# Loading a token block by column halves and splitting the copies of its turned tiles between two engines

## The chip, the core and the metric

The kernel runs on one core of one Trainium2 chip. The metric is the device time of one launch in microseconds (us). Five engines work beside each other and meet through semaphores: TensorE (PE, matmuls and weight loads), VectorE (DVE), ScalarE (ACT), GpSimd (POOL) and SyncE (SP), which here only issues transfers. Matmul results land in eight banks (bank 0 to 7) that DVE and ACT read.

## The reference

One inference step of a two-layer encoder for 256 prompt tokens and 64 sample tokens, 320 in all, of width 1024 (float32):

```python
x = [x_prompt (256, 1024); x_sample (64, 1024)]
for i in range(2):
    h = rmsnorm(x, ln_mix_pre[i])                   # x / sqrt(mean(x^2) + eps) * g
    mix = attention(h @ w_att_in) @ w_att_out       # i = 0: forgetting and window attention
    mix = mlstm(h @ w_rec_in) @ w_rec_out           # i = 1
    x = x + rmsnorm(mix, ln_mix_post[i])
    x = x + rmsnorm(conv_ffn(rmsnorm(x, ln_ffn_pre[i])), ln_ffn_post[i])
    x = x + sigmoid(x @ w_ple_gate[i]) * (p[i] @ w_ple[i])
```

Only the first step matters here: x comes in by rows (tokens), is turned so that features lie on the partitions, is multiplied by the norm's gain, and meets the first columns of w_att_in. The factor 1/sqrt(mean) is applied later, to the results of the matmuls.

## The kernel before

**Data.** The turned x, `xT`, is eight tiles j = 0 to 7 of 128 features by 320 tokens. Every float32 product is made of three faster ones: an operand is split into a high part (`hH` for x times gain, `wh` for weights) that ACT writes as a rounded copy, and a low part (`hL`, `wl`) that DVE gets by subtracting. A weight *unit* is 1024 by 128 numbers (512 KB) in one of R = 4 slots: SP loads it into `raw`, ACT makes `wh` (`hi(u)`), DVE makes `wl` (`lo(u)`), then PE uses it for 24 matmuls.

**The start.** SP issues three loads of x into `xtok` (tokens on the partitions, whole rows of 4 KB, all counted by `ld_x`), then unit 0, unit 1 and so on; unit u waits for `lo(u-4)`. ACT issues five small loads of the norms' gains (`nrow`). PE first does WARM = 16 throwaway matmuls on constants, then waits for all of x, and turns tile after tile (`turn_rows`, three transposes each, against an identity); between tile 1 and tile 2 it turns the gains (`parameters(1)`, which waits for `nrow`), and behind each of the tiles 3 to 7 stand three more throwaway matmuls. DVE copies each turned tile from its bank to `xT` (`x_in(j)`) and the gains to `NC` (`par_in(1)`). ACT multiplies (`hH`), DVE makes `hL` (`prenorm_lo`).

**The first projections.** `ahead` runs units 0 and 1 together, feature tile by feature tile k: four matmuls that need `hH[k]`, then two that need `hL[k]`; its first one needs `lo(1)`. Then come unit 2 (`in_unit`), inside which, before its k = 5, stands `stats`: matmuls that add up the squares of x over the partitions. It waits until DVE has added the squares of tiles 0 to 6 (`add_squares`), which ACT made with `Square`. From there DVE (`ms`), POOL (`rcol`, the inverse root), DVE (`diag`), PE (`spread_rms`, inside unit 3) and DVE (`rstd`) make the factor by which all results of the projections are multiplied.

**What sets the order.** Each engine's program is written out by hand and runs in its order; an instruction that waits holds up all behind it. ACT: `hi(0)`, four `hH`, `hi(1)`, four `hH`, `hi(2)`, four squares, `hi(3)`, four squares, the narrow weights `wnH` (which wait for a transfer of POOL's queue, whose first transfer waits for unit 2's landing), some small ones, `hi(4)`. DVE: the copies of tiles with `lo(0)` and `lo(1)` between them, eight `hL`, `lo(2)`, `lo(3)`, six additions of squares, `ms`, `lo(4)`, `diag`, `lo(5)`, `rstd`. The banks are given out by `group_banks`, in turn over banks 0 to 3 for these groups.

Of the kernel before, what the change touches and what calls it, by code (L numbers as in the profile page):

```python
# [21 lines left out]
P = 128  # L22
# [30 lines left out]
WARM = 16  # L53
# [78 lines left out]
def group_banks():  # L132

    fixed = {("pt_e", 7): 4, ("pt_o", 7): 5, ("pt_s", 7): 6}
    fixed.update({("o", s): 7 for s in range(8)})
    upper = ("rows", "spread", "W", "Y", "Cs")
    banks, turn, last, previous = [], [0, 0], {}, []
    for n, key in enumerate(group_order()):
        b = fixed.get(key)
        if b is None:  # L140
            k = int(key[0] in upper)
            b = 4 * k + turn[k] % 4
            turn[k] += 1
        banks.append(b)
        previous.append(last.get(b))
        last[b] = n
    return banks, previous
# [16 lines left out]
def encoder_step(nc, I, O):  # L164
    ctx = ExitStack()
    with ctx:
# [168 lines left out]
        for name, signal, n in (("x", "x_in", 8), ("pe", "pe_f", 4), ("in0", "in_read0", 18),  # L335
                                ("narrow0", "narrow_step0", 1), ("vt", "vt_read", 5), ("kt", "kt_read", 5), ("lf", "lf_read", 1),
                                ("pt_e", "pt_e", 8), ("pt_o", "pt_o", 8), ("pt_s", "pt_s", 8), ("o", "o_lo0", 8), ("in1", "in_read1", 24),
                                ("narrow1", "narrow_step1", 1), ("rows", "rows_read", 1), ("spread", "sdec", MH), ("W", "P", MH), ("ktok", "Kg", MH),
                                ("vtok", "vtok_read", 8), ("Y", "Yn", 12), ("Cs", "C_new", MH), ("Cp", "Cp", MH), ("heads", "mo_f", 8)):
            read_by(name, signal, n)  # L340
# [63 lines left out]
        def _(sp):  # L404
            sp.dma_start(xtok[:, 0, :], I["x_prompt"][0, 0:P]).then_inc(sem("ld_x"), 16)
            sp.dma_start(xtok[:, 1, :], I["x_prompt"][0, P:TP]).then_inc(sem("ld_x"), 16)
            sp.dma_start(xtok[0:TS, 2, :], I["x_sample"][0]).then_inc(sem("ld_x"), 16)
# [10 lines left out]
            for l in range(2):  # L418
                w_in, cols, w_out = (I["w_att_in"], ATT_COLS, I["w_att_out"]) if l == 0 else (I["w_rec_in"], REC_COLS, I["w_rec_out"])
                for i, c in enumerate(cols):  # L420
                    load(UNITS[f"in{l}"] + i, col_unit(w_in[0], c))
                for i in range(8):
# [232 lines left out]
        def _(pe):  # L655
# [83 lines left out]

            for i in range(WARM):  # L740
                mmul(bank[7][:, 0:P], ones[:], ident[:], start=True, stop=True)  # L741
            pe.wait_ge(sem("ld_x"), 48)
            for j in range(KT):
                gi = gid("x", j)
# [5 lines left out]
                if j >= 3:  # L750
                    for i in range(3):
                        mmul(bank[7][:, 0:P], ones[:], ident[:], start=True, stop=True)
# [408 lines left out]
        def _(act):  # L1161
# [69 lines left out]
            def input_attention():  # L1231
                for j in range(KT):
                    act.wait_ge(sem("x_in"), j + 1)
                    if j == 0:
                        act.wait_ge(sem("par_in"), 1)
                    A(hH[:, j, :], xT[:, j, :], ACT.Copy, scale=NC[:, 0, 64 + j:65 + j]).then_inc(sem("h_hi"), 1)
                    if j == 3:
                        hi(1)
# [231 lines left out]
        def _(dve):  # L1470
# [138 lines left out]
            def input_attention():  # L1609
# [5 lines left out]
                def x_in(j):  # L1615
                    gi = gid("x", j)
                    bank_full(dve, gi)
                    V.tensor_copy(xT[:, j, :], gbank(gi)[:, 0:T]).then_inc(sem("x_in"), 1)

                x_in(0)  # L1620
                x_in(1)
                par_in(1)
                x_in(2)
                x_in(3)
                lo(0)
                x_in(4)
                x_in(5)
                lo(1)
                x_in(6)
                prenorm_lo("mixpre0", 0, 0, 64)  # L1630
                x_in(7)
                for j in range(1, 8):
                    prenorm_lo("mixpre0", 0, j, 64)
# [357 lines left out]
```

## Time and profile before

| | us |
|---|---|
| median of three runs | 1091.24 |
| lowest and highest | 1090.67 and 1092.66 |
| the profiled execution | 1091.82 |
| its span, from the first instruction to the last | 1090.1 |
| PE busy | 1073.3 |
| DVE busy | 674.6 |
| ACT busy | 534.9 |
| POOL busy | 253.5 |

The span is what the rows of the profile cover; 1.7 us of the profiled execution lie around it. Times in rows count from the span's start. A PE that is busy is not always at its full rate, since a matmul's row also covers its wait in the pipeline.

### The profile page before, as it was taken

Reading aid. Unit: us, or ns where it says so; the run is one execution under the profiler, and the core shown is the slowest. Engines: PE = TensorE matmul, PEld = TensorE weight load, DVE = VectorE, ACT = ScalarE, POOL = GpSimd, SP = SyncE. Lnnn points to the kernel's source line nnn. Section 1 sums busy time; section 2 is a strip of 40 time slices with the busy share of each in tenths; the row PEclk is TensorE's granted clock in tenths of the full one; section 3 lists DMA queues with packets and bytes.
Section 4 is the critical chain, followed back from the end, with each engine's and each line's share of the span. In section 5 each row is a group of like instructions: output and inputs, shape, how many; then the busy total and the mean of one; then the engine's idle time right before and its main releaser. Section 6 shows DMA issues by size and latency. Waiting matters only on the chain.

```text
span 1090.1 us, 20380 instructions
## 1 busy us (share of the span) xinstructions
PE 1073.3 (98%) x7343; PEld 1043.8 (96%) x7343; DVE 674.6 (62%) x1232; ACT 534.9 (49%) x932; POOL 253.5 (23%) x384
## 2 busy tenths in 40 slices
PE   9999999999999999999999999999999999999998
PEld 8889989999999999999999889899999999999998
DVE  5876547777777753334876655567777777433364
ACT  5465455555555543334656444545555555433353
POOL 5600036222333210002410102432223332100020
PEclk9999999999999999999999999999999999999999
DMA  9623252555555545554555334355555555455441
GB/s 238 169 72 98 87 155 72 169 156 164 146 151 154 153 141 152 155 152 126 136 148 135 97 100 127 103 113 159 162 163 144 148 153 153 143 152 152 149 122 50
DMA packets 281926, 150.39 MB, mean 138 GB/s; under 512 B 5592, under 2 KB 278816, under 8 KB 281872
## 3 DMA queue, kind: packets, MB, share of 16 engines
q1 hardware_dynamic: 279184, 144.20, 47.0%
q0 software_dynamic: 2544, 5.40, 1.7%
q8 instruction: 37, 0.61, 0.2%
q14 instruction: 17, 0.14, 0.0%
q10 hardware_dynamic: 144, 0.05, 0.0%
HBM read 145.54 MB, written 4.08 MB: 137 GB/s over the span
## 4 chain that ended last, share of the span: by engine, by line
PE 94%; DVE 3%; POOL 2%; ACT 1%; issue 0%; DVEq 0%; POOLq 0%; ACTq 0%
PE bank L662 27%; PE bank L664 27%; PE bank L663 27%; PE bank L686 2%; PE bank L689 1%; PE bank L704 1%; PE bank L1038 1%; DVE wl L1481 1%; PE bank L726 1%; DVE hidden_lo L1944 1%; PE bank L712 1%; PE bank L741 1%; PE bank L929 1%; POOL sqb L393 1%; PE bank L890 0%
## 5 line engine op out<-in xcount | busy, mean ns | idle before, releaser
L1481 DVE TENSOR_TENSOR wl<-raw,wh 128x1024 fp32r<-128x1024 f32 x270 | 332.4, 1232 | 253.2 <-ACT wh L1178 251.3
L662 PE MATMUL bank<-hH,wh 128*128 128x320 f32 x1280 | 399.7, 312 | 1.1 <-DVE mix L1530 1.0
L664 PE MATMUL bank<-hH,wl 128*128 128x320 f32 x1280 | 396.1, 309 | 0.0
L663 PE MATMUL bank<-hL,wh 128*128 128x320 f32 x1280 | 396.0, 309 | 0.0
L1178 ACT ACTIVATE wh<-raw 128x1024 fp32r<-128x1024 f32 x270 | 284.4, 1055 | 190.6 <-PE bank L664 175.1
L662 PEld LDWEIGHTS bank<-hH,wh 128*128 128x128 f32 x1280 | 240.7, 188 | 4.6 <-issue 2.7
L663 PEld LDWEIGHTS bank<-hL,wh 128*128 128x128 f32 x1280 | 240.8, 188 | 0.0
L664 PEld LDWEIGHTS bank<-hH,wl 128*128 128x128 f32 x1280 | 240.8, 188 | 0.0
L662 PE MATMUL bank<-hidden_hi,wh 128*128 128x320 f32 x720 | 223.4, 310 | 0.5 <-ACT mix L1369 0.5
L664 PE MATMUL bank<-hidden_hi,wl 128*128 128x320 f32 x720 | 222.5, 309 | 0.0
L663 PE MATMUL bank<-hidden_lo,wh 128*128 128x320 f32 x720 | 222.5, 309 | 0.0
L662 PEld LDWEIGHTS bank<-hidden_hi,wh 128*128 128x128 f32 x720 | 135.1, 188 | 1.3 <-ACT mix L1369 0.8
L663 PEld LDWEIGHTS bank<-hidden_lo,wh 128*128 128x128 f32 x720 | 135.2, 188 | 0.0
L664 PEld LDWEIGHTS bank<-hidden_hi,wl 128*128 128x128 f32 x720 | 135.1, 188 | 0.0
L635 POOL TENSOR_TENSOR fb<-cv,us 128x256 f32<-128x256 f32 x64 | 44.3, 692 | 312.4 <-DVE us L1924 188.9
L393 POOL TENSOR_TENSOR sqb<-sqb 128x320 f32<-128x320 f32 x42 | 43.4, 1034 | 203.8 <-ACT sqb L1420 146.2
L1405 ACT ACTIVATE cv<-cv 128x322 f32<-128x322 f32 x64 | 30.3, 474 | 99.7 <-DVE cv L1919 99.7
L1919 DVE SCALAR_TENSOR_TENSOR cv<-gp,PC,cv 128x322 f32<-128x322 f32 x128 | 70.6, 552 | 7.8
L1409 ACT ACTIVATE hidden_hi<-fb 128x320 f32 (+1 forms) x64 | 30.2, 472 | 78.2 <-POOL cs L639 78.2
L639 POOL COPY cs<-gp 128x4 f32 x64 | 62.0, 968 | 0.0
L1928 DVE TENSOR_TENSOR hidden_lo<-fb,hidden_hi 128x320 f32 (+1 forms) x64 | 31.4, 490 | 43.4 <-ACT hidden_hi L1409 43.4
L1402 ACT ACTIVATE cv<-gp,PC 128x322 f32<-128x322 f32 x64 | 42.1, 658 | 26.5 <-DVE gp L1911 26.1
(374 smaller groups left out, 1060.0 us busy)
## 6 DMA issues: line engine op xcount, KB each, us to landing
raw<-in_w_ffn_up SPq DMA_DIRECT2D x128, 512.0 KB, 4.1
raw<-in_w_ffn_down SPq DMA_DIRECT2D x64, 512.0 KB, 3.9
raw<-in_w_rec_in SPq DMA_DIRECT2D x24, 512.0 KB, 3.9
raw<-in_w_att_in SPq DMA_DIRECT2D x18, 512.0 KB, 4.9
raw<-in_w_ple_gate SPq DMA_DIRECT2D x16, 512.0 KB, 4.1
raw<-in_w_att_out SPq DMA_DIRECT2D x8, 512.0 KB, 3.7
raw<-in_w_rec_out SPq DMA_DIRECT2D x8, 512.0 KB, 3.9
raw<-in_w_ple SPq DMA_DIRECT2D x4, 512.0 KB, 3.5
```

The lines of the kernel that those rows point to most:

```text
L393: ops.tensor_tensor(sqb[:, 0, :], sqb[:, 0, :], sqb[:, j, :], ALU.add).then_inc(sem("sq_added"), 1)
L635: g.tensor_tensor(fb[:, s, 0:TP], cv[:, s, 0:TP], us[:, s, 0:TP], ALU.mult)
L639: g.tensor_copy(dst, tail).then_inc(sem(f"f{l}"), 1)
L662: mmul(out, a, rh[:, k, :], start=first, stop=False)
L663: mmul(out, a, rl[:, k, :], start=False, stop=False)
L664: m = mmul(out, b, rh[:, k, :], start=False, stop=last)
L1178: A(wh[:, u % R, :], raw[:, u % R, :], ACT.Copy).then_inc(hi_ready, 1)
L1402: A(cv[:, s, :], gp[:, s, 2:T + 4], ACT.Identity, scale=PC[:, l, bass.ds(j + 64, 1)], bias=PC[:, l, bass.ds(j + 96, 1)]).then_inc(sem(f"cv ...
L1405: A(cv[:, s, :], cv[:, s, :], ACT.Gelu_apprx_tanh).then_inc(sem(f"gelu{l}"), 1)
L1481: V.tensor_tensor(wl[:, u % R, :], raw[:, u % R, :], wh[:, u % R, :].bitcast(F32), ALU.subtract).then_inc(lo_ready, 1)
L1919: V.scalar_tensor_tensor(out=cv[:, s, :], in0=gp[:, s, tap:tap + T + 2], scalar=PC[:, l, bass.ds(j + 32 * tap, 1)], in1=cv[:, s, :], op0=A ...
L1928: V.tensor_tensor(FL[:, bass.ds(j, 1), :].rearrange("p a t -> p (a t)"), fb[:, s, :], FH[:, bass.ds(j, 1), :].rearrange("p a t -> p (a t)" ...
```

## The change

- x is loaded by halves of its columns. SP issues both prompt blocks' first 512 columns as one load and the sample's as another (`ld_x0`), then unit 0, then the other halves (`ld_x1`), then unit 1. Rows are now 2 KB long. PE waits for the first half before tile 0 and for the second before tile 4.
- WARM goes from 16 to 9. Behind tiles 4 to 7 stand two throwaway matmuls each, behind tile 3 none: 8 in place of 15. They write bank 3 in place of bank 7.
- The turned tiles use banks 4 to 7 (tile j in bank 4 + j % 4), a tile waiting for the copy of the tile four before it. The first projections keep their banks 1, 2, 3 and 0.
- DVE copies the even tiles (`x_even`), ACT the odd ones (`x_odd`). On both engines the copies now stand among `hi`, `lo`, `hH` and `hL`; `hL` of tile 1 is made before tile 6 is copied.

```diff
-WARM = 16
+WARM = 9
...
+    fixed.update({("x", j): 4 + j % 4 for j in range(KT)})
...
-            sp.dma_start(xtok[:, 0, :], I["x_prompt"][0, 0:P]).then_inc(sem("ld_x"), 16)
-            sp.dma_start(xtok[:, 1, :], I["x_prompt"][0, P:TP]).then_inc(sem("ld_x"), 16)
-            sp.dma_start(xtok[0:TS, 2, :], I["x_sample"][0]).then_inc(sem("ld_x"), 16)
+            def load_x(half):
+                landed = sem(f"ld_x{half}")
+                c = slice(half * 512, (half + 1) * 512)
+                sp.dma_start(xtok[:, 0:2, c], I["x_prompt"][0].rearrange("(t p) d -> p t d", p=P)[:, :, c]).then_inc(landed, 16)
+                sp.dma_start(xtok[0:TS, 2, c], I["x_sample"][0][:, c]).then_inc(landed, 16)
...
+                if l == 0:
+                    load_x(0)
                 for i, c in enumerate(cols):
                     load(UNITS[f"in{l}"] + i, col_unit(w_in[0], c))
+                    if (l, i) == (0, 0):
+                        load_x(1)
...
-            for i in range(WARM):
-                mmul(bank[7][:, 0:P], ones[:], ident[:], start=True, stop=True)
-            pe.wait_ge(sem("ld_x"), 48)
+            def throwaway(n):
+                for i in range(n):
+                    mmul(bank[3][:, 0:P], ones[:], ident[:], start=True, stop=True)
+
+            throwaway(WARM)
             for j in range(KT):
+                if j % 4 == 0:
+                    pe.wait_ge(sem(f"ld_x{j // 4}"), 32)
                 gi = gid("x", j)
                 bank_free(pe, gi)
                 turn_rows(gi, T, lambda t, n: xtok[0:n, t, :], j)
                 if j == 1:
                     pe.wait_ge(sem("ld_norms0"), 16 * 5)
                     parameters(1)
-                if j >= 3:
-                    for i in range(3):
-                        mmul(bank[7][:, 0:P], ones[:], ident[:], start=True, stop=True)
+                if j >= 4:
+                    throwaway(2)
```

ACT's order at the start, before the change. `wh<-raw` is `hi`, `hH<-xT,NC` a tile times its gain:

```order
L1178 ACTIVATE wh<-raw 128x1024 [waits raw_landed0]
L1236 ACTIVATE hH<-xT,NC 128x320 [waits par_in,x_in]
L1236 ACTIVATE hH<-xT,NC 128x320 [waits x_in] x3
L1178 ACTIVATE wh<-raw 128x1024 [waits raw_landed1]
L1236 ACTIVATE hH<-xT,NC 128x320 [waits x_in] x4
L1178 ACTIVATE wh<-raw 128x1024 [waits raw_landed2]
```

The same place of the change, up to `hH` of tile 2; `xT<-bank5` and `xT<-bank7` are the copies of tiles 1 and 3:

```order
L1190 ACTIVATE wh<-raw 128x1024 [waits raw_landed0]
L1248 ACTIVATE xT<-bank5 128x320 [waits bank_done5]
L1252 ACTIVATE hH<-xT,NC 128x320 [waits x_even,par_in]
L1190 ACTIVATE wh<-raw 128x1024 [waits raw_landed1]
L1248 ACTIVATE xT<-bank7 128x320 [waits bank_done7]
L1252 ACTIVATE hH<-xT,NC 128x320 [waits x_odd]
L1252 ACTIVATE hH<-xT,NC 128x320 [waits x_even]
```

Behind these follow the copy of tile 5, `hH` of 3 and 4, the copy of tile 7, `hH` of 5, 6 and 7, and `hi(2)` as before. `hi(1)` moved from behind four `hH` to behind one, so ten instructions stand between it and `hi(2)` in place of four.

DVE's order before, from the copy of tile 3 on; `wl<-raw,wh` is `lo`, `hL<-xT,NC,hH` is `prenorm_lo`:

```order
L1618 COPY xT<-bank0 128x320 [waits bank_done0]
L1481 TENSOR_TENSOR wl<-raw,wh 128x1024 [waits hi_ready]
L1618 COPY xT<-bank1 128x320 [waits bank_done1]
L1618 COPY xT<-bank2 128x320 [waits bank_done2]
L1481 TENSOR_TENSOR wl<-raw,wh 128x1024 [waits hi_ready]
L1618 COPY xT<-bank3 128x320 [waits bank_done3]
L1485 SCALAR_TENSOR_TENSOR hL<-xT,NC,hH 128x320 [waits h_hi]
L1618 COPY xT<-bank0 128x320 [waits bank_done0]
L1485 SCALAR_TENSOR_TENSOR hL<-xT,NC,hH 128x320 [waits h_hi] x7
L1481 TENSOR_TENSOR wl<-raw,wh 128x1024 [waits hi_ready] x2
```

And in the change, from the copy of tile 0 on:

```order
L1646 COPY xT<-bank4 128x320 [waits bank_done4]
L1641 COPY NC<-bank0 128x96 [waits bank_done0]
L1509 TENSOR_TENSOR wl<-raw,wh 128x1024 [waits hi_ready]
L1646 COPY xT<-bank6 128x320 [waits bank_done6]
L1509 TENSOR_TENSOR wl<-raw,wh 128x1024 [waits hi_ready]
L1513 SCALAR_TENSOR_TENSOR hL<-xT,NC,hH 128x320 [waits h_hi]
L1646 COPY xT<-bank4 128x320 [waits bank_done4]
L1513 SCALAR_TENSOR_TENSOR hL<-xT,NC,hH 128x320 [waits h_hi]
L1646 COPY xT<-bank6 128x320 [waits bank_done6]
L1513 SCALAR_TENSOR_TENSOR hL<-xT,NC,hH 128x320 [waits h_hi] x6
L1509 TENSOR_TENSOR wl<-raw,wh 128x1024 [waits hi_ready] x2
```

Four copies left DVE's queue, and `lo(1)` stands ahead of the copies of tiles 4 and 6.

## Rows read from the trace of the kernel before

**Rows 1.** The page: busy time, and shares of the chain that ended last.

```profile
PE 1073.3 (98%) x7343; PEld 1043.8 (96%) x7343; DVE 674.6 (62%) x1232; ACT 534.9 (49%) x932; POOL 253.5 (23%) x384
PE 94%; DVE 3%; POOL 2%; ACT 1%; issue 0%; DVEq 0%; POOLq 0%; ACTq 0%
```

**Rows 2.** The chain in order of time: start, us, what.

```profile
2.10 6.63 PE bank L741 x32
...
10.95 0.86 PE bank L752 x6
11.82 0.42 PE bank L726 x3
```

**Rows 3.** Landings: the three loads of x, then unit 0, unit 1.

```profile
L407 SPq DMA_DIRECT2D xtok<-in_x_sample x1: 576/576/576, 1.7 to 1.7; - x1
...
DMA to landing us min/median/max: 3.9/5.1/6.5
...
L416 SPq DMA_DIRECT2D raw<-in_w_att_in x1: 578/578/578, 2.3 to 2.3; - x1
...
DMA to landing us min/median/max: 7.3/7.3/7.3
...
L416 SPq DMA_DIRECT2D raw<-in_w_att_in x1: 758/758/758, 3.0 to 3.0; - x1
...
DMA to landing us min/median/max: 8.5/8.5/8.5
```

**Rows 4.** Order of time, DVE: start, us, what, [idle before].

```profile
16.54 3.32 DVE L1485 SCALAR_TENSOR_TENSOR hL<-xT,NC,hH 128x320 fp32r<-128x320 f32 x7
19.78 2.35 DVE L1481 TENSOR_TENSOR wl<-raw,wh 128x1024 fp32r<-128x1024 f32 x2
22.05 3.48 DVE L393 TENSOR_TENSOR sqb<-sqb 128x320 f32<-128x320 f32 x6
...
29.64 0.79 DVE L1495 TENSOR_SCALAR cv<-ident,rcol 128x128 f32<-128x128 f32 x3 [0.79 <-POOL rcol L500]
...
32.14 0.49 DVE L1500 COPY rstd<-bank 128x320 f32<-128x320 f32 x1 [0.59 <-PE bank L712]
```

**Rows 5.** The same for ACT.

```profile
10.62 1.91 ACT L1236 ACTIVATE hH<-xT,NC 128x320 fp32r<-128x320 f32 x4
12.44 1.04 ACT L1178 ACTIVATE wh<-raw 128x1024 fp32r<-128x1024 f32 x1
...
17.13 1.05 ACT L1178 ACTIVATE wh<-raw 128x1024 fp32r<-128x1024 f32 x1
...
19.52 1.04 ACT L1178 ACTIVATE wh<-raw 128x1024 fp32r<-128x1024 f32 x1
...
24.91 0.31 ACT L1245 ACTIVATE wnH<-wnr 128x128 fp32r<-128x128 f32 x1 [2.90 <-DMA wnr<-in_w_rec_in]
...
26.55 1.99 ACT L1178 ACTIVATE wh<-raw 128x1024 fp32r<-128x1024 f32 x2
```

**Rows 6.** ACT's copy of a 128x320 result from a bank, later in layer 0.

```profile
L1229 ACT ACTIVATE hidden_hi<-bank x8: 417/424/438, 63.5 to 134.0; 128x320 fp32r<-128x320 f32 x8
```

**Rows 7.** Order of time, PE's weight loads: first of the projections, first of `stats`.

```profile
16.69 0.19 PEld L686 LDWEIGHTS bank<-hH,wh 128*128 128x128 f32 x1
...
25.89 1.45 PEld L704 LDWEIGHTS bank<-ones,sqb 128*128 128x128 f32 x12
```

**Rows 8.** Windows of 1 us: busy (count) of PE, PEld, DVE, ACT, POOL; PEclk, DMA, GB/s.

```profile
4.00:5.00 1.00, 1.00 (x6) 1.00 (x6) 0.00 (x0) 0.34 (x1) 0.78 (x4) 1.00 1.03 402
...
9.00:10.00 1.00, 1.00 (x7) 0.64 (x7) 0.73 (x2) 0.34 (x1) 0.00 (x0) 1.00 1.20 290
```

**Rows 9.** Throwaway matmuls from 2 to 7.75 us; then two windows of 3.4 us.

```profile
L741 PE MATMUL bank<-ident,ones 128*128 128x128 f32 x26 | 5.9, 427 | 2.1 <-POOL ones L476 2.1
...
161.60:165.00 3.40, 1.30 (x10) 0.90 (x8) 3.30 (x8) 2.48 (x7) 1.50 (x2) 1.00 0.38 113
165.00:168.40 3.40, 3.40 (x13) 3.40 (x14) 3.08 (x5) 2.76 (x8) 3.32 (x4) 0.50 0.02 5
```

More of the change, by code:

```diff
@@ L334, in encoder_step @@
             READ[gid("cache", i)] = ("cache_read", n + 1)
-        for name, signal, n in (("x", "x_in", 8), ("pe", "pe_f", 4), ("in0", "in_read0", 18),
+        for j in range(KT):
+            READ[gid("x", j)] = (("x_even", "x_odd")[j % 2], j // 2 + 1)
+        for name, signal, n in (("pe", "pe_f", 4), ("in0", "in_read0", 18),
                                 ("narrow0", "narrow_step0", 1), ("vt", "vt_read", 5), ("kt", "kt_read", 5), ("lf", "lf_read", 1),
@@ L1231, in input_attention, with x_odd, x_normed @@
             def input_attention():
[L1232 to L1235, printed above, removed]
-                    A(hH[:, j, :], xT[:, j, :], ACT.Copy, scale=NC[:, 0, 64 + j:65 + j]).then_inc(sem("h_hi"), 1)
-                    if j == 3:
-                        hi(1)
+                def x_odd(j):
+                    gi = gid("x", j)
+                    bank_full(act, gi)
+                    A(xT[:, j, :], gbank(gi)[:, 0:T], ACT.Copy).then_inc(sem("x_odd"), 1)
+                def x_normed(j):
+                    act.wait_ge(sem(("x_even", "x_odd")[j % 2]), j // 2 + 1)
+                    A(hH[:, j, :], xT[:, j, :], ACT.Copy, scale=NC[:, 0, 64 + j:65 + j]).then_inc(sem("h_hi"), 1)
+                x_odd(1)
+                act.wait_ge(sem("par_in"), 1)
+                x_normed(0)
+                hi(1)
+                x_odd(3)
+                x_normed(1)
+                x_normed(2)
+                x_odd(5)
+                x_normed(3)
+                x_normed(4)
+                x_odd(7)
+                for j in range(5, KT):
+                    x_normed(j)
                 hi(2)
@@ L1613, in par_in, with x_even @@
                     V.tensor_copy((PC, NC)[i % 2][:, i // 2, 0:n], gbank(gid("par", i))[:, 0:n]).then_inc(sem("par_in"), 1)
-                def x_in(j):
+                def x_even(j):
                     gi = gid("x", j)
                     bank_full(dve, gi)
-                    V.tensor_copy(xT[:, j, :], gbank(gi)[:, 0:T]).then_inc(sem("x_in"), 1)
-                x_in(0)
-                x_in(1)
+                    V.tensor_copy(xT[:, j, :], gbank(gi)[:, 0:T]).then_inc(sem("x_even"), 1)
+                x_even(0)
                 par_in(1)
-                x_in(2)
-                x_in(3)
                 lo(0)
-                x_in(4)
-                x_in(5)
+                x_even(2)
                 lo(1)
-                x_in(6)
                 prenorm_lo("mixpre0", 0, 0, 64)
-                x_in(7)
-                for j in range(1, 8):
+                x_even(4)
+                prenorm_lo("mixpre0", 0, 1, 64)
+                x_even(6)
+                for j in range(2, 8):
                     prenorm_lo("mixpre0", 0, j, 64)
```

## The prediction

> **What bounds the kernel now.** The page first: PE is busy for 1073.3 of the span's 1090.1 us and holds 94% of the chain that ended last [rows 1]. So time is won only where PE waits or does work that the result doesn't need. The chain in order of time shows such a place at the start: 16 throwaway matmuls from 2.10 for 6.63 us, then per turned tile 0.42 us of transposes, and from tile 3 on 0.86 us of throwaways for each [rows 2]. The first projection's weights load at 16.69 [rows 7]. All of x is in `xtok` at 1.7 + 6.5 = 8.2 [rows 3], just before the throwaways end (8.7), so at first sight PE's own queue sets the start, and the change shortens exactly that.
>
> The second look goes to what the projections need next. From the first projection to `stats` PE runs 25.89 - 16.69 = 9.20 us without a stop [rows 7]. `stats` needs DVE's six additions of squares, which end at 22.05 + 3.48 = 25.53 [rows 4]. PE comes to them 0.36 us after they are ready. That is all the lead the other engines have: if PE starts its projections x us sooner and the additions don't move, PE waits x - 0.36 us inside unit 2, and `rstd`, on which all results of the projections wait, is hardly sooner. So the question is not when PE starts, but when the additions end.
>
> **The change part by part, PE.** In the first 5.65 us 26 halves of throwaway matmuls start, 0.21 us each [rows 9] (a float32 matmul is two instructions; this is the half clock, 1.2 GHz, since later six take 0.86, 0.14 each [rows 2]). Nine matmuls, 18 halves: 3.8 us, so they end at 5.9. The first half of x is 640 KB; before, 512 KB had landed at 0.8 + 3.9 = 4.7 and 1 MB at 1.3 + 5.1 = 6.4 [rows 3], so it lands between 5.1 (by bytes) and 6.4. I take 5.9. Tiles 0 and 1 follow at once. The gains have no landing in the profile; their last load stands about beside unit 0's, which landed at 2.3 + 7.3 = 9.6, and I take that as the latest for them. Tiles 2 and 3 are then turned at 11.0 at the latest. The second half of x is complete when 1.25 MB of x and unit 0 are, the same bytes that were in at 9.6 before. Tiles 4 to 7 with two throwaways each take 0.42 + 0.57 = 1.0 us apiece at full clock: tile 7 is turned by 14.5, give or take 0.5, and PE is ready for the projections by then. It was 16.69.
>
> **ACT.** Here is what the change costs. `hi(1)` needs unit 1, which landed at 3.0 + 8.5 = 11.5 [rows 3]. The same 2.25 MB stand ahead of and in it in the change, so I leave it there. Before, ACT did four `hH` first and `hi(1)` at 12.44 didn't wait. Now it stands behind one `hH`, waits until 11.5, and behind it are queued seven `hH` and three copies. In a stream one `hH` takes (1.91 - 0.55)/3 = 0.45 us and one `hi` 1.99 - 1.05 = 0.94 [rows 5]. A copy from a bank is 0.42 long alone [rows 6] against `hH`'s 0.55, so I take 0.40 in a stream (bounds 0.33 and 0.45: 0.4 us over three). Sum: 11.5 + 0.94 + 3 x 0.40 + 7 x 0.453 = 16.8 for `hi(2)`. One wait comes on top: `hH` of tile 4 needs DVE's copy of it, which stands behind `lo(1)` and one `hL`: `hi(1)` ends at 12.54, `lo(1)` takes 1.13 and `hL` 0.46 in a stream [rows 4], the copy ends at about 14.7, and ACT would be there at 14.6. With 0.15 for it `hi(2)` starts at 16.95, in place of 17.13. The four squares and `hi(3)` keep their distance, 19.52 - 17.13 = 2.39: `hi(3)` ends at 16.95 + 2.39 + 1.04 = 20.4, before 20.56. So ACT, which had idled between `hH` for want of tiles, is now full, and gains 0.2 us only.
>
> **DVE.** It was bound by itself: `lo(3)` started at 19.78 + 1.13 = 20.91, 0.35 after `hi(3)` ended [rows 4, 5]. With four copies fewer it has its last `hL` behind it at about 18.3, `lo(2)` at 19.5, and waits for `hi(3)`. `lo(3)` starts at 20.5, the additions 1.14 later and end 3.48 after that: 25.1. PE loads the weights of `stats` at 25.15 in place of 25.89: **0.74 us sooner**.
>
> **What PE does meanwhile.** Its projections need `lo(1)`, over at 13.8, and start there, 2.9 us sooner than before; 9.2 later it is at `stats`, at 23.0, and waits 2.1 us. What the change says it does on PE is done, and three quarters of it is given back there.
>
> **Behind that.** `stats`, `ms`, `rcol`, `diag`, the nine blocks of matmuls ahead of `spread_rms`: all follow from `stats` and move with it. One tie is new if the gain is larger: `lo(4)` needs `hi(4)` (26.55 to 27.6), which stands behind `wnH`, which waited 2.90 us for its transfer until 24.91 [rows 5]. DVE waited 0.79 before `diag` and 0.59 before `rstd` [rows 4], 1.38 together. With `wnr` landing as before `rstd` can't come more than 1.4 us sooner, however early the squares are. For 0.74 the tie is slack. The bank moves cost nothing: the projections keep their banks and lose a wait.
>
> **Sum.** 1091.82 (the profiled execution, span and 1.7 around it) - 0.74 = 1091.1; against the median of the runs, 1091.24, it is 1090.5.
>
> **Rivals.**
> 1. *Loads late, ACT later still* (0.15). Every 0.1 us by which unit 1 lands later goes straight into the additions. x now comes in rows of 2 KB. Rows of 4 KB moved at 402 GB/s, weights' rows of 512 B at 290 [rows 8]. If 2 KB rows moved as slowly as the latter, 1.31 MB would take 4.5 in place of 3.3 us: unit 1 at 12.7, `stats` at 26.35, 0.5 us later than before: 1091.7. If a copy takes 0.45, add 0.15.
> 2. *Start carried through* (0.10). Unit 1 lands sooner (at the 402 and 290 GB/s of [rows 8], 2.36 MB would take 3.3 + 3.6 = 6.9 us and not the 8.5 from issue to landing, so there is some slack for another order of loads to find), and `wnr` too. Then 1.4 us with the tie, at most 2.9 with nothing in the way: 1089.8 to 1088.3. Against it: both must come together, and the bytes ahead of unit 1 are the same.
> 3. *Half clock* (0.15), the case that ends slower. Before, PE was busy without a break from 2.10, and up to 7.75 at least its matmuls kept the half clock's 0.21 us; and much later, after a stretch of 3.4 us in which it was busy for 1.30, the granted clock was 0.50 for the next 3.4 [rows 9]. In the change PE stops at 5.9 or after tile 1, while still at half clock. If it stays so, a tile takes up to 0.84 and two throwaways 0.84: from 9.6 or 10.5 tile 7 is turned at about 16.4 in place of 14.5, 1.3 after ACT wants to copy it, and the additions end at 26.4. The projections start near 17.3, and each us of them at half clock adds half a us. `stats` at 26.6 to 28.5: 0.7 to 2.6 later, middle 1.3: 1092.5. It decides from the point where PE starts its projections after 25.15 - 9.2 = 15.95, or tile 7 after 15.1; up to there the wait of 2.1 us swallows it (4 us of matmuls at half clock).
> 4. *Not what it says*: the first half lands no sooner than 8.2 (its sample part late, as before). Then tile 3 is turned by 11, tile 7 by 15.0, and the result is the forecast's.
>
> The Trainium skill (TensorE: Matmul & The Clock Gate, Part 4: PE-mode transpose) says that matmuls in transpose mode don't count as busy for the clock. By that rule the tiles would not help to raise it and rival 3 would be the likely case, 1092.5. In this trace PE did nothing but transposes from 8.7 to 10.9 (seven instructions in the window from 9 to 10 at a granted clock of 1.00 [rows 8]) and was not slowed; that speaks to keeping the clock, not to getting it. So I leave the rival at 0.15.
>
> **How the numbers follow.** Forecast (with rival 4) 0.60, rivals 1 to 3 0.15, 0.10, 0.15. Time 1090.5. Every mechanism moves less than 3 us of 1091, while three runs of one kernel spread over 2 us; 0.2%, 2.2 us, is about what can be told from no change. The range takes rival 2's tied end and rival 3's middle, and 0.5 us on either side for the runs' own spread: 1089.0 to 1093.0. Faster by over 0.2% needs rival 2 without the tie, or its tied end with luck in the runs: 0.10. Slower needs rival 3 at its far end: 0.10. Same: 0.80.
>
> **What would show it.** Right: transposes from about 6 us, ACT idle before `hi(1)` until 11.5 with a DMA as the releaser, projections from 13.8, PE idle some 2 us before `stats` with DVE's additions as the releaser, `lo(3)` waiting for ACT, `rstd` at 31.4. The first wrong step would show as a landing of unit 1 off 11.5, or as throwaways behind tile 4 still 0.21 apart. If PE doesn't wait at `stats`, the argument is wrong as a whole.

## The result, and the profile after

| | median us | range | runs |
|---|---|---|---|
| before | 1091.72 | 1090.35 to 1092.77 | 20 |
| changed | 1093.63 | 1091.86 to 1096.15 | 20 |

Ratio 1.0020, 95% interval 1.0013 to 1.0026: the change makes the kernel 0.2% slower. Forecast were 1090.5 us and a range of 1089.0 to 1093.0, so both missed.

The profiled execution of the changed kernel took 1092.07 us, with a span of 1090.4 in place of 1090.1. It is one of the quick ones of its 20. First the page, busy time and then the shares of the chain that ended last (compare [rows 1]).

```profile
PE 1071.8 (98%) x7315; PEld 1041.6 (96%) x7315; DVE 672.8 (62%) x1228; ACT 536.1 (49%) x936; POOL 252.8 (23%) x384
PE 93%; DVE 3%; POOL 1%; ACT 1%; DMA 1%; issue 0%; SPq 0%; DVEq 0%; POOLq 0%; ACTq 0%
```

PE does 28 instructions less (14 throwaway matmuls), yet nothing is won. A DMA is new in the chain. The chain in order of time (start, us, what) says which one, and stands against [rows 2].

```profile
3.21 7.39 DMA xtok<-in_x_sample
10.64 0.64 PE bank L735 x3
...
12.34 1.07 PE bank L751 x4
13.41 0.72 PE bank L735 x3
...
16.61 0.58 PE bank L695 x4
...
25.84 1.50 PE bank L713 x12
```

The start is now bound by a load: the second half of x. Behind it, `x3` of turned tiles take 0.72 us at 13.41, where [rows 2] have 0.42, and two throwaways 1.07. The landings, of that load and then of unit 1, the last line of each being us from issue to landing (compare [rows 3]):

```profile
L412 SPq DMA_DIRECT2D xtok<-in_x_sample x1: 682/682/682, 3.2 to 3.2; - x1
...
DMA to landing us min/median/max: 7.4/7.4/7.4
...
L421 SPq DMA_DIRECT2D raw<-in_w_att_in x1: 587/587/587, 3.9 to 3.9; - x1
...
DMA to landing us min/median/max: 8.2/8.2/8.2
```

So the second half of x was in at 3.2 + 7.4 = 10.6 and unit 1 at 12.1. Now stretches of the start, and one much later: busy us (count) of PE, PEld, DVE, ACT, POOL, then granted clock, DMA, GB/s (compare [rows 8, 9]).

```profile
2.00:5.60 3.60, 3.51 (x16) 3.51 (x17) 0.00 (x0) 1.28 (x1) 2.85 (x13) 1.00 0.93 272
5.60:8.20 2.60, 2.60 (x17) 1.61 (x15) 0.75 (x2) 0.34 (x1) 2.30 (x7) 1.00 1.09 338
8.20:10.60 2.40, 0.02 (x1) 0.00 (x0) 1.63 (x2) 1.49 (x3) 0.55 (x1) 1.00 1.17 255
10.60:12.40 1.80, 1.76 (x11) 1.29 (x12) 0.00 (x0) 0.24 (x1) 0.00 (x0) 1.00 1.20 290
12.40:15.80 3.40, 3.40 (x14) 2.62 (x14) 2.55 (x5) 3.24 (x7) 1.56 (x3) 0.50 1.11 269
15.80:26.00 10.20, 10.20 (x70) 9.86 (x70) 8.61 (x16) 9.14 (x22) 5.66 (x9) 1.00 0.98 250
162.60:169.40 6.80, 5.90 (x21) 5.50 (x22) 6.42 (x11) 6.09 (x17) 5.80 (x6) 0.50 0.02 6
```

Three readings. PE stands still from 8.2 to 10.6, with tiles 0 to 3 turned and tile 4 not there. Soon after, from 12.4, its granted clock is 0.50 (1.2 GHz) for 3.4 us. And near 165 us the kernel spends 6.8 us at half clock, where before it was 3.4 [rows 9]. Note the first row: the column says 1.00, but a matmul takes 3.51 / 16 = 0.22 us there; at the very start one has to read the durations.

What ACT and DVE do meanwhile (start, us, what, [idle before]); ACT first (compare [rows 5]), then DVE (compare [rows 4]), then PE's weight loads (compare [rows 7]).

```profile
12.16 1.06 ACT L1190 ACTIVATE wh<-raw 128x1024 fp32r<-128x1024 f32 x1 [2.47 <-DMA raw<-in_w_att_in]
...
17.70 1.04 ACT L1190 ACTIVATE wh<-raw 128x1024 fp32r<-128x1024 f32 x1
...
20.09 1.05 ACT L1190 ACTIVATE wh<-raw 128x1024 fp32r<-128x1024 f32 x1
```

```profile
21.17 1.23 DVE L1509 TENSOR_TENSOR wl<-raw,wh 128x1024 fp32r<-128x1024 f32 x1 [1.06 <-ACT wh L1190]
22.31 3.48 DVE L396 TENSOR_TENSOR sqb<-sqb 128x320 f32<-128x320 f32 x6
...
32.06 0.49 DVE L1528 COPY rstd<-bank 128x320 f32<-128x320 f32 x1 [0.68 <-PE bank L721]
```

```profile
16.34 0.19 PEld L695 LDWEIGHTS bank<-hH,wh 128*128 128x128 f32 x1
...
25.84 1.30 PEld L713 LDWEIGHTS bank<-ones,sqb 128*128 128x128 f32 x11 [0.26 <-DVE sqb L396]
```

ACT waits 2.47 us for unit 1 with its queue behind it, and DVE now waits for ACT, both as forecast. But the additions end at 25.79, where 25.53 was before. `stats` comes at 25.84 against 25.89, `rstd` at 32.06 against 32.14. This execution, then, has won 0.08 us up to `rstd`, and lost 0.4 later. That is not the loss of 1.9 us in the medians. The mean granted clock of the runs points to the rest: it was 0.990 or 0.992 in 14 of the 20 runs of the changed kernel, and in none of the 131 runs of before beside the experiments below (a 132nd, of 1161.0 us at 0.848, was in a slow state and is left out here and in the ratios). The profiled execution had 0.994. A mean of 0.992 instead of 0.997 is 0.005 x 1090 x 2 = 11 us more at half clock. The main question is where these lie, and which part of the change brings them.

The mean doesn't tell all. One of the 20 runs took 1095.38 us at 0.997, and such runs come back below: 3 of 10 at 1094.98 to 1095.35 in the second experiment, and 2 of 10 at 1094.99 and 1095.30 where the kernel before gets WARM = 9. All six have 9 throwaways ahead. The 71 runs of before at 0.997 end at 1092.49, and no other run at 0.997 took more than 1093.41. Since the column misses the half clock at the very start, a start that stays at half clock for longer would fit, but no profile fell on such a run: it stays open.

### The profile page after: what moved, and what is told of

Same layout as the page of the kernel before. It is cut to its first block, busy times and chain, and to the rows that moved or that the text cites. A ratio compares the mean times of both kernels' runs of the same rounds, so it can differ in the third digit from the quotient of the medians.

```text
span 1090.4 us, 20328 instructions
## 1 busy us (share of the span) xinstructions
PE 1071.8 (98%) x7315; PEld 1041.6 (96%) x7315; DVE 672.8 (62%) x1228; ACT 536.1 (49%) x936; POOL 252.8 (23%) x384
## 4 chain that ended last, share of the span: by engine, by line
PE 93%; DVE 3%; POOL 1%; ACT 1%; DMA 1%; issue 0%; SPq 0%; DVEq 0%; POOLq 0%; ACTq 0%
PE bank L671 27%; PE bank L673 27%; PE bank L672 27%; PE bank L695 2%; PE bank L698 1%; PE bank L713 1%; PE bank L1050 1%; DVE wl L1509 1%; PE bank L721 1%; DMA xtok<-in_x_sample 1%; DVE hidden_lo L1969 1%; PE bank L735 1%; PE bank L941 1%; POOL sqb L396 1%; PE bank L902 0%
```

## The experiments

Two theories. *Clock*: with fewer throwaways PE stops at the start before or shortly after it has the full clock, and then runs at 1.2 GHz through turned tiles and projections; the loads and copies matter little. *Loads*: x by halves lands late, and with it unit 1, so ACT and the additions come late; the throwaways matter little. All times are medians in us, with the ratio to the kernel before on the same chip. Each edit is against the changed kernel, unless a line says otherwise.

### The old throwaways in the changed kernel

```diff
-WARM = 9
+WARM = 16
-                if j >= 4:
-                    throwaway(2)
+                if j >= 3:
+                    throwaway(3)
```

> The changed kernel with the throwaway matmuls of before: 16 ahead of the tiles, 3 behind each of tiles 3 to 7. Loads, banks and copies stay changed. Theory A (the loss is the clock: PE stands still while it waits for x, falls to half clock, and the stop costs more than the shorter queue gains): PE is busy from 2.1 until the second half of x has landed, no stretch at half clock after about 8 us; projections start near 17.0, stats near 26.2, so 1092.0, at most 0.5 above the kernel before, and 1.5 below the changed one. Theory B (the loss is the later landing of unit 1, 12.16 in the profile after against 11.5, with more work queued behind it on ACT): throwaways don't matter, 1093.6 as the changed kernel.

Measured: 1092.78, ratio 1.0008 (0.9999 to 1.0017). The profiled run had no stretch at half clock up to 163 us, and the 11 runs had means of 0.994 to 0.997. Yet its second half of x landed at 11.4 and `hi(1)` started at 12.88, so that the additions ended at 26.33 and `stats` came at 26.39. The low mean clocks are gone, and of the 1.79 us that the changed kernel lost on this chip (1093.74 against 1091.95) 0.96 come back. How much is only roughly known: the interval overlaps that of the changed kernel beside it (1.0005 to 1.0023). What is left, 0.08%, isn't told from nothing by its interval.

### The new throwaways in the kernel before

```diff
# against the kernel before
-WARM = 16
+WARM = 9
-                if j >= 3:
-                    for i in range(3):
+                if j >= 4:
+                    for i in range(2):
```

> The kernel before with the throwaways of the change alone: 9 ahead of the tiles, 2 behind tiles 4 to 7. Theory A (clock): PE stands still from 5.9 until x lands at 8.2 and is at half clock for part of the start; 1093.3 to 1094.5, about as slow as the changed kernel or slower. Theory B (unit 1's landing and ACT's queue): loads and ACT are as before, seven throwaways less on PE can only help: 1090.7 to 1091.7.

Measured: 1094.13, ratio 1.0024 (1.0014 to 1.0033), without any of the new loads and copies. The windows of its profiled run, columns as above:

```profile
6.00:8.20 2.20, 0.77 (x5) 0.31 (x4) 0.00 (x0) 0.00 (x0) 1.97 (x6) 1.00 1.15 241
8.20:10.20 2.00, 2.00 (x12) 1.23 (x13) 1.64 (x4) 0.78 (x1) 0.58 (x1) 0.99 1.20 289
10.20:20.40 10.20, 10.20 (x39) 8.41 (x40) 8.29 (x16) 7.67 (x16) 7.10 (x11) 0.50 1.13 275
```

PE has little to do from 6.0 to 8.2, where it waits for x, and 2 us later it is at half clock for 10.2 us. `stats` came at 27.99 and `rstd` at 34.24, 2.1 later than before. Fewer throwaways alone can cost as much as the whole change. But this stop, before the first tile, is one that the changed kernel doesn't have: its first half was in at 5.2. The changed kernel's stop is at tile 4.

### The changed kernel once more

> The changed kernel as it is, for a second profile and on the same chip as the others. Both theories: 1093.6. Theory A: the profile shows a stretch at half clock in the first 20 us, perhaps at another place than the first profile's 12.4 to 15.8, and stats follows it; where the half clock lies later, stats comes later than the first profile's 25.8. Theory B: the stretch at half clock is at the same cost as before and stats stands at 25.5 to 26 whatever the clock does.

Measured: 1093.74, ratio 1.0014 (1.0005 to 1.0023); 7 of its 11 runs had a mean clock of 0.992. This time the profile fell on one of those. Its windows, then its chain:

```profile
6.50:9.90 3.40, 2.33 (x14) 1.30 (x13) 2.10 (x4) 1.83 (x3) 2.17 (x4) 1.00 1.12 316
9.90:13.40 3.50, 3.50 (x14) 2.60 (x15) 1.11 (x2) 1.93 (x4) 0.00 (x0) 0.50 1.20 290
13.40:20.10 6.70, 6.70 (x27) 5.80 (x27) 5.86 (x12) 5.37 (x12) 6.55 (x10) 0.50 1.15 292
20.10:28.00 7.90, 7.90 (x57) 7.90 (x55) 4.63 (x9) 6.49 (x15) 0.68 (x2) 1.00 0.67 158
```

```profile
3.20 6.58 DMA xtok<-in_x_sample
9.83 0.94 PE bank L735 x3
10.78 1.15 PE bank L751 x4
...
17.55 1.07 PE bank L695 x4
18.61 0.53 PE bank L698 x2
...
21.41 0.59 PE bank L695 x4
```

Here x came sooner than in the first profile (9.8 in place of 10.6), and ACT had unit 1 at 11.47, just as forecast. PE waited for the second half of x for 0.97 us only. The result is nevertheless worse: half clock for 10.2 us, 9.9 to 20.1. The same four matmuls of a projection take 1.07 at 17.55 and 0.59 at 21.41. The additions ended at 26.21, but PE came to `stats` only at 27.70, and `rstd` stood at 33.95, 1.8 later than before. At 1093.93 us this execution is of the medians' kind, and the first profile was a lucky one.

### Throwaways that fill the stop at tile 4

```diff
-                if j >= 4:
-                    throwaway(2)
+                if j >= 3:
+                    throwaway(8 if j == 3 else 3)
```

> The changed kernel with its PE idle time filled: 9 throwaways ahead of the tiles as in the change, 8 behind tile 3 (while the second half of x is awaited), 3 behind tiles 4 to 7. Theory A: the clock is kept wherever it had risen, projections near 16, stats at 25.8 or just ahead of it because ACT and the additions bind there: 1091.2 to 1092.0. Theory B: 1093.6 as the changed kernel.

Measured: 1093.04, ratio 1.0014 (1.0004 to 1.0023), a miss in size: by its times it isn't told from the unchanged kernel beside it, which has the same ratio. What it shows is on the clock: with 9 throwaways ahead as in the change, and only the stop at tile 4 filled, the profiled run kept the full clock to 163 us, and none of the 11 runs had a mean under 0.994 (the unchanged one beside it: 7 of 11 at 0.992). So it is what lies between tile 3 and tile 4 that brings the granted half clock, for executions like the second profile at least. (A third throwaway behind each later tile came with it. In the second profile the clock had already fallen at 9.9, so those can't be what would have kept it there; in the first it fell at 12.4, behind tile 4, and for that one they are not ruled out.) In its profile the start was late by the loads: the second half landed at 11.3, `hi(1)` started at 12.87, `stats` at 26.36, and `rstd` came at 32.58, 0.44 later than before. That is less than half of the 1.09 us between the medians, and 4 of the 11 runs took 1093.97 to 1095.21 at means of 0.994 or 0.995. What those lost isn't shown.

### The loads, one by one

```diff
# against the first experiment: each row of x whole, as before
-            def load_x(half):
...
+            sp.dma_start(xtok[:, 0, :], I["x_prompt"][0, 0:P]).then_inc(sem("ld_x"), 16)
+            sp.dma_start(xtok[:, 1, :], I["x_prompt"][0, P:TP]).then_inc(sem("ld_x"), 16)
+            sp.dma_start(xtok[0:TS, 2, :], I["x_sample"][0]).then_inc(sem("ld_x"), 16)
...
-                if j % 4 == 0:
-                    pe.wait_ge(sem(f"ld_x{j // 4}"), 32)
+                if j == 0:
+                    pe.wait_ge(sem("ld_x"), 48)
```

> The changed kernel with the throwaways of before (16, and 3 behind tiles 3 to 7) and the loads of before (three loads of whole rows of x ahead of unit 0). What stays changed are the banks, the copies on two engines and the place of hi(1). Theory C (splitting the loads makes unit 1 land later, and that went into the additions of squares): unit 1 lands at 11.5, hi(2) starts at about 17.0 and the additions end at 25.1 as the prediction worked out; PE's own queue then sets stats at 25.9, so 1091.7 to 1092.0, the kernel before's time. Theory D (the copies on ACT and hi(1)'s place are late whatever the loads do): the additions end at 26 or later, 1092.5 and more.

Measured: 1093.0, ratio 1.0008 (0.9999 to 1.0017), the same as with halves, and by its median what theory D says. Five runs lay at 1091.4 to 1092.0 and six at 1093.0 to 1093.6. The profiled run, one of the lower, had `hi(1)` at 11.12, the additions over at 25.50 (theory C had 25.1) and `rstd` at 31.77. What separates the two groups stayed open.

The other way round, only the loads by halves, in the kernel before:

```diff
# against the kernel before
+                if l == 0:
+                    load_x(0)
                 for i, c in enumerate(cols):
                     load(UNITS[f"in{l}"] + i, col_unit(w_in[0], c))
+                    if (l, i) == (0, 0):
+                        load_x(1)
```

> The kernel before with the loads by halves alone (first halves, unit 0, second halves, unit 1), PE waiting for each half; throwaways, banks and copies as before. Theory C: unit 1 lands at 12.2 to 12.9 as in the profiles of the changed loads; hi(1) stood at 12.44 on ACT anyway, so at most 0.5 later; 1091.7 to 1092.3. If instead the halves cost nothing, unit 1 at 11.5 and 1091.9.

Measured: 1091.71, ratio 0.9998 (0.9990 to 1.0007). The loads alone cost nothing, where the old order of ACT and 16 + 15 throwaways stand over them.

### ACT's order: `hi(1)` behind three more pieces

```diff
# against the first experiment
                 x_normed(0)
-                hi(1)
                 x_odd(3)
                 x_normed(1)
                 x_normed(2)
+                hi(1)
```

> Run e1_old_throwaways with hi(1) moved on ACT behind the copy of tile 3 and hH of tiles 1 and 2, which ACT can do while it would wait for unit 1. Theory (hi(1) waiting at the head of ACT's queue delays the additions, which set stats in e1 at 26.39): hi(2) starts 1.2 sooner, near 17.0, the additions end near 25.1, stats follows PE's queue at about 25.8; 1091.9, 0.6 to 0.9 below e1. Rival (stats in e1 is not set by ACT): 1092.8 as e1.

Measured: 1091.93, ratio 1.0000 (0.9991 to 1.0009). The profile doesn't bear out why it should be sooner: `hi(2)` started at 18.49, not at 17.0, and `stats` came at 26.63. Unit 1 landed at 13.1 there, and behind `hi(1)` ACT waited 1.38 us for DVE's copy of tile 4, which stands behind `lo(1)` and so behind `hi(1)` itself: what was moved ahead of `hi(1)` didn't shorten that chain. A miss in its steps; the difference to 1.0008 is within the intervals.

### Two fewer throwaways per tile with whole rows: a stop at `stats`

The order of the last one, 16 throwaways, x by whole rows, two behind tiles 4 to 7.

> The version that the findings point to: changed banks and copies, loads of x by whole rows as before, 16 throwaways ahead of the tiles, two behind each of tiles 4 to 7 as in the change, hi(1) behind the copy of tile 3 and hH of tiles 1 and 2. PE is busy without a stop from 2.1 on. If the clock is kept: projections near 15.3, additions end near 24.7, stats near 24.8 to 25.0, 0.9 sooner than before: 1091.0. If fewer throwaways lose the clock even without a stop: 1093 and more.

Measured: 1094.19, ratio 1.0024 (1.0014 to 1.0034), though the loads were in time. Then a kernel that differs by `x_even(2)` ahead of `lo(0)` on DVE:

> e8_rows_two_later with DVE's copy of tile 2 moved ahead of lo(0), since in e8 ACT waited 1.4 us for it with hi(1) queued behind. ACT's chain should end 1.3 sooner: hi(2) near 16.7, additions end near 24.7, PE at stats at 24.2, so it waits 0.5 in place of 2.0. Theory A (every stop of PE in the start can cost the clock): no half clock before 160 us in most runs, rstd near 31.2, 1091.0, the fastest so far. Rival (two throwaways behind a tile are themselves too few for the clock): 1093 and more as e8.

Measured: 1093.5, ratio 1.0022 (1.0012 to 1.0031). ACT's wait of 1.38 us was still there, since it was for the copy of tile 4, as above. The edit moved the wrong instruction. And a third, with PE's wait at `stats` filled:

```diff
# against the first of these three
-                in_unit(0, 2, lambda k: stats("mixpre0") if k == 5 else None)
+                def filled_stats(k):
+                    if k == 5:
+                        for i in range(8):
+                            mmul(bank[7][:, 0:P], ones[:], ident[:], start=True, stop=True)
+                        stats("mixpre0")
+
+                in_unit(0, 2, filled_stats)
```

> e8_rows_two_later with eight throwaway matmuls ahead of stats (0.22 us each, 1.8 us), where PE stood still for 2.0 us in e8 before its clock fell at 27.9. Their bank is free by then. Theory A: no half clock at 27.9, stats at 26.2 as in e8, 1092.0 to 1092.5, 2 below e8. Rival (the clock fell for another reason, or e8 is slow for another): 1094 as e8.

Measured: 1092.01, ratio 1.0005 (0.9996 to 1.0014). Windows of the first and of the third, in this order:

```profile
24.40:26.40 2.00, 0.24 (x3) 0.20 (x2) 1.68 (x4) 1.82 (x7) 0.00 (x0) 1.00 1.03 258
26.40:27.90 1.50, 1.50 (x14) 1.50 (x14) 0.17 (x2) 1.50 (x2) 0.00 (x0) 0.99 0.17 50
27.90:31.30 3.40, 3.40 (x15) 3.40 (x14) 2.61 (x5) 1.29 (x2) 3.32 (x4) 0.50 0.33 78
```

```profile
24.40:26.40 2.00, 2.00 (x19) 1.89 (x18) 1.69 (x5) 1.46 (x6) 0.00 (x0) 1.00 1.19 291
...
27.90:31.30 3.40, 3.40 (x24) 3.40 (x24) 2.60 (x6) 1.66 (x2) 3.14 (x4) 1.00 0.28 77
```

In the first PE is busy for 0.24 of 2.0 us at `stats`, and from 27.9 does 15 matmuls at half clock. In the third, with eight useless matmuls in that place, it does 24 at full clock in the same 3.4 us. `rstd` came at 33.94 and at 32.59.

But the stop doesn't always bring the half clock. The profiled execution of the second kernel (1092.04 us) has the same stop of 2.0 us, and then the full clock, 26 matmuls in 3.4 us, and `rstd` at 32.11:

```profile
23.90:25.90 2.00, 0.25 (x3) 0.01 (x1) 1.69 (x5) 1.93 (x7) 0.00 (x0) 1.00 1.06 271
...
27.90:31.30 3.40, 3.40 (x26) 3.40 (x25) 2.61 (x5) 1.06 (x1) 3.40 (x5) 1.00 0.43 118
```

In 4 of its 10 runs the mean clock was 0.993 or lower, in none of the 11 of the third. By the medians the stop costs 2.2 us against the first, 1.5 against the second, which ran beside the third. The intervals of these two overlap a little (1.0012 to 1.0014). It is a stop in the place, and of the length, of the 2.1 us that the prediction counted as free.

### The two counts of throwaways apart, in the kernel before

```diff
# against the kernel before
-WARM = 16
+WARM = 9
```

> The kernel before with 9 in place of 16 throwaways ahead of the tiles, nothing else. PE stands still from 5.9 until x lands at 8.2. Theory A: half clock in part of the start, but three throwaways behind each tile bring it back sooner than in e2; 1092.5 to 1094. Without an effect of the clock PE starts the tiles at 8.2 and it is 1091.7.

Measured: 1094.96, ratio 1.0029 (1.0020 to 1.0039).

```profile
6.00:8.70 2.70, 0.42 (x3) 0.25 (x3) 0.00 (x0) 0.00 (x0) 2.46 (x6) 1.00 1.16 250
8.70:15.50 6.80, 6.80 (x27) 4.89 (x27) 3.75 (x7) 4.58 (x7) 1.99 (x5) 0.50 1.00 244
```

A stop of 2.3 in 2.7 us before the first tile, and then 6.8 us at half clock. `stats` was at 28.52. So in the kernel before all of the second experiment's loss comes from 9 in place of 16. The other count alone:

```diff
# against the kernel before
-                if j >= 3:
-                    for i in range(3):
+                if j >= 4:
+                    for i in range(2):
```

> The kernel before with two throwaways behind tiles 4 to 7 in place of three behind tiles 3 to 7, nothing else. PE stays busy up to the projections, which start near 15.2; the additions of squares end near 25, so PE waits 0.5 to 1 us at stats. Theory A: the short wait costs the clock in few runs; 1091.0 to 1092.0. If two behind a tile are too few in themselves: 1093 and more.

Measured: 1090.83, ratio 0.9996 (0.9987 to 1.0005), the lowest median of all, though 0.7 us below the kernel before is within the interval. The projections started at 14.72 in place of 16.69, and PE waited for the additions:

```profile
PEld bank L704 <- DVE sqb L393: 0.6, 1, 0.6
```

`stats` came at 24.56, `rstd` at 30.79, 1.35 sooner, with the full clock kept. It is the mechanism of the forecast, from one part of the change, and its size is near the tie of 1.4 us that the prediction names.

Filling that wait of 0.6 with three throwaways:

> e12_before_two_behind (the kernel before with two throwaways behind tiles 4 to 7, which looked fastest: 1090.83) with three throwaways ahead of stats, 0.66 us, about the 0.6 that PE stood still there. stats stays at 24.6. 1090.5 to 1091.1; if the short stop cost no clock, the same as e12.

Measured: 1091.04, ratio 0.9996 (0.9987 to 1.0005). No difference: this wait of 0.6 us needs no filling.

### 16 throwaways in the changed kernel, without and with a filled stop at `stats`

> The changed kernel with 16 throwaways ahead of the tiles in place of 9, nothing else. PE's stop in front of tile 4 shrinks from 2.4 us to about 0.5 (it ends tile 3 at 10.4, not 8.2), and the stop at stats grows, as PE no longer runs at half clock. If the front stop is nearly all of the loss: 1092.0 or less, few runs with a mean granted clock of 0.992 or lower. If the stop at stats costs as much as in e8: 1093.0 to 1094.2.

Measured: 1093.54, ratio 1.0014 (1.0005 to 1.0023). The stop at tile 4 was gone in its profile and projections started at 14.94, but PE waited 1.2 us at `stats` until 25.41, and was at half clock from 28.2 to 31.6. `rstd` came at 33.17. Behind a further wait, of 1.4 us for `mix`, there were 3.4 us more at half clock from 41.9. The median lies in the range named for a stop at `stats` that costs as much as with whole rows.

> e13_warm16 with eight throwaways ahead of stats: both stops are closed, the loads by halves, banks and copies stay as in the change. If the stops of PE are the cause of the loss: 1091.7 to 1092.3 (stats at 26.0 to 26.4, set by the additions), no run at 0.992. If something else in the loads or copies is part of it: 1092.8 and more.

Measured: 1095.45, ratio 1.0038 (1.0024 to 1.0051), from five runs of 1091.14 to 1097.03: a miss. The profiled one was the quickest, with the second half at 9.5, unit 1 at 11.1, `stats` at 25.36 and `rstd` at 31.58, 0.56 sooner than before. It shows what the change could give when x lands by the forecast, not what it mostly gives. By the test set beforehand, 1092.8 and more, something else in the loads or copies is part of the loss. The same kernel was profiled three times more, for a late execution.

> The kernel of e14_warm16_stats_filled again, whose profiled execution took 1091.14 while its four others took 1094.8 to 1097.0 at mean granted clocks of 0.991 to 0.994. If PE still stops for long somewhere in the first 60 us in most executions, this profile shows a stretch at half clock there and what PE waited for; 1095. If e14's slow executions were of another kind (nothing at half clock beyond that of the kernel before), the profile shows stats and rstd in place and the time lost elsewhere.

Measured: 1093.46, ratio 1.0018 (1.0008 to 1.0027); x at 11.0, `stats` at 26.30, `rstd` at 32.52, no half clock up to 165 us. Again the loss isn't all clock as the mean shows it: 8 of the 10 runs had 0.994 to 0.997, and took 1092.56 to 1094.04.

> A further profile of the same kernel, in case e16's execution is again one of the quick ones: 1095 with a stretch at half clock in the first 60 us, or 1091 without.

Measured: 1098.89 in one execution, the late one. Its chain and its windows:

```profile
3.21 8.61 DMA xtok<-in_x_sample
...
30.07 1.78 PE bank L803 x16
31.86 1.23 PE bank L713 x12
```

```profile
9.80:12.00 2.20, 0.14 (x1) 0.15 (x2) 1.62 (x2) 0.99 (x3) 0.00 (x0) 1.00 1.14 261
...
12.30:22.60 10.30, 10.30 (x40) 8.85 (x41) 7.04 (x12) 8.03 (x17) 7.23 (x11) 0.50 0.94 249
```

The second half of x came at 11.8; PE stood still for 2.1 of 2.2 us before it, and then ran at half clock for 10.3 us. The eight fillers, needed by nobody, then took 1.78 us on the path. The weights of `stats` load at 31.59. Against the profile before it, x is 0.8 later and `stats` 5.3. So 16 throwaways don't close the stop at tile 4 when x is late.

> As e17: a further profile of the same kernel, 1095 with a stretch at half clock in the first 60 us, or 1091 without.

Measured: 1092.7; x at 9.9, `stats` at 25.14, `rstd` at 31.36, 0.78 sooner than before, and 10.2 us at half clock near 165 us in place of 3.4, an estimated 3.4 us of matmuls at most, which can have taken the gain back.

## Why the prediction was wrong

**Where it was right.** ACT's queue behind `hi(1)`: the wait for unit 1 is there (2.47 us), and DVE waits for ACT in place of being bound by itself. The pitches hold: `hi(1)` to `hi(2)` is 5.54 measured, 16.95 - 11.5 = 5.45 predicted; `hi(2)` to `hi(3)` is 2.39 in both. That a gain on PE stops at the additions is shown by the kernel before with two throwaways behind a tile: projections 1.97 us sooner, `rstd` 1.35.

**Landings.** "The second half of x is complete when 1.25 MB of x and unit 0 are, the same bytes that were in at 9.6 before." It was in at 10.6, and over eleven profiles of kernels with halves at 9.5 to 11.8, never sooner by more than 0.1. Unit 1 was taken at 11.5, and came at 12.1 here, 11.4 in the second profile. This is the term of the additions that was mis-sized: 0.66 late in a forecast gain of 0.74, and 25.79 for 25.1. In the first profile it turned the gain to nothing; it didn't make the loss of the second, where unit 1 was in time. The gains, taken at 9.6 at the latest, were in by 6.9 and 7.6, so that tile 3 was turned at 8.2 and 8.9, far ahead of the 11.0 allowed for it.

**The clock, the step that failed.** Rival 3 stood at 0.15, since the row "speaks to keeping the clock, not to getting it". So the sum put the clock at nothing. Half clock in the start is what 21 of the changed kernel's 31 runs point to by their mean, at the size named: `stats` forecast at 26.6 to 28.5 under it, 27.70 in the second profile, and 1.3 us named for it against 1.9 between the medians. That the size fits is in part luck, for the rival's mechanism is not what the profiles show. It has PE stop "while still at half clock" and stay there. In both profiles the full clock had come before the first stop (six transposes in 1.16 us at 5.84 in the first and at 7.70 in the second, as in the kernel before), and was lost behind it. I had weighed the rival by what PE does (transposes) and not by where it stops. The prediction has its front stop after tile 1, for the gains; the real one is in front of tile 4, for the second half of x, and lasts 2.4 or 1.0 us. For this stop, the filled one shows the place: same 9 throwaways ahead, eight plain matmuls between tiles 3 and 4, no half clock in the start. For the one at `stats`, the filled `stats` shows it, with whole rows: 1.5 to 2.2 us. That a stop ahead of the first tile costs as much was shown in the kernel before (9 in place of 16: 1.0029).

**Transposes and the clock.** The Trainium skill (TensorE: Matmul & The Clock Gate, Part 4: PE-mode transpose) says that matmuls in transpose mode don't count as busy for the clock. By that rule rival 3 would have been the likely case. The second profile agrees with it: PE is busy for 2.33 of 3.4 us from 6.5, mostly on transposes, and at half clock from 9.9. That a wait of only 0.97 us lies in it speaks for the rule, too. But the fillers between tiles 3 and 4, which cure it, are plain matmuls and close the wait at once, and no run does one without the other, so none tells the rule from the stop. The stops at `stats` have no transposes near them, and there the stop alone was followed by half clock (27.9 to 31.3 behind the one of 2.0 us).

**"Up to there the wait of 2.1 us swallows it".** A wait hides what PE loses before it, but it isn't free: with PE at rest for 2.0 us from 24.4 the clock was half from 27.9 in one profile, and stayed full in another. Had all loads come as forecast, the changed kernel would likely have had this stop still, as the one with 16 throwaways did (`stats` at 25.41 and `rstd` 33.17, 1.0 later than before). The 2.1 us themselves don't follow from the prediction's own figures: it has tile 7 turned by 14.5 and yet starts the projections at 13.8. From 14.5 the wait is 25.15 - 9.20 - 14.5 = 1.45 us.

**The tie of 1.4 us and the range.** Slower got 0.10 since only rival 3's far end was put there; its middle, 1092.5, was the top of the range but for 0.5 us of spread. With the rival likely, it should have been the forecast.

**What stays open.** With the old throwaways, the changed copies stand at 1.0008 (0.9999 to 1.0017), with halves and with whole rows. Nothing here decides whether these 0.9 us are real. With 16 throwaways and a filled `stats` the changed kernel still stood at 1.0018 and 1.0038, and late landings of x, as in the profile of 1098.89, can explain part of it. No profile fell on one of the runs of 1095 us at a mean of 0.997. Nor was the cause of the spread in the landings found, or that of the two groups of runs with whole rows.

## What to carry to other kernels

Useless matmuls at a kernel's start are no surplus because PE waits behind them: before taking some away, list each place where PE would then stand still, and price a stretch at half clock behind it (here 3.4 to 10.3 us of it, behind stops of 1.0 to 2.4 us, and none behind one of 2.0). Compare times and mean granted clock over many runs and not one profile; here the first profile showed 0.3 us of a loss of 1.9. And a stop may not be the whole loss: with 16 throwaways ahead and `stats` filled this kernel was still slow in most runs. A start that gets its gain from a load landing just in time should be priced at the late end of that load's landings, since the early end gives a few tenths and the late one costs microseconds.

## What the runs showed of the hardware

- The same load, second half of x (issued at 3.2), took 6.3 to 8.6 us to land from one execution to the next. Before, the three loads of all of x took 3.9 to 6.5 [rows 3].
- Where and how long the clock falls differs between executions of one kernel: 12.4 to 15.8 in the first profile of the changed kernel, 9.9 to 20.1 in the second.
- The same stop of 2.0 us at `stats` was followed by 3.4 us at half clock in one profile (27.9 to 31.3) and by none in that of a nearly equal kernel. Waits of 0.5 to 0.7 us at tile 4 or `stats` were followed by none.
- Near 165 us, behind a stretch in which PE is partly idle [rows 9], half clock lasted 3.4 us before, 6.8 in the changed kernel's profile, and 10.2 in the last profile, with nothing changed in the kernel there. It is a part of the runs' spread: 3.4 us more at half clock are, as an estimate, up to 1.7 us of matmuls. Whether the start has a say in it, no run here shows.
